# A sum over features before a projection: one fp32 product on TensorE against a split on GpSimd and two ordinary products

## The reference, cut to what matters

```python
def _rmsnorm(x, g):
    xf = x.astype(jnp.float32)
    y = xf * lax.rsqrt(jnp.mean(xf * xf, axis=-1, keepdims=True) + EPS) * g.astype(jnp.float32)
    return y.astype(x.dtype)
...
    x = x + merged @ w_out
    ffn, new_conv = _conv_ffn(_rmsnorm(x, norm_ffn), conv_state, w_up, conv_w, conv_b, w_down)
    x = x + ffn
```

## Time and profile before

| what | us |
|---|---|
| median of 3 runs | 1532.3 |
| lowest, highest | 1532.28, 1532.6 |
| the profiled execution, its own time | 1532.53 |
| its span in the profile | 1530.7 |
| TensorE busy | 1522.8 (99%) |
| VectorE busy | 1025.8 (67%) |
| ScalarE busy | 667.2 (44%) |
| GpSimd busy | 469.4 (31%) |
| granted clock of TensorE, mean | 0.999 |

### The profile page before, as it was taken

One profiled execution on the slowest core, in us unless ns is written; L12 is line 12 of the kernel. 1 busy time (PEld: TensorE's weight loads), 2 busy tenths in 40 slices (PEclk: granted clock), 3 DMA queues, 4 the chain that ended last, 5 costly groups with the idle time before them and its releaser, 6 DMA issues.

```text
span 1530.7 us, 33612 instructions
## 1 busy us (share of the span) xinstructions
PE 1522.8 (99%) x12350; PEld 1508.1 (99%) x12350; DVE 1025.8 (67%) x1479; ACT 667.2 (44%) x903; POOL 469.4 (31%) x608
## 2 busy tenths in 40 slices
PE   9999999999999999999999999999999999999998
PEld 9999999999999999999999999999999999999998
DVE  7655889887667676567777777777777764444443
ACT  7344445454667544444333333333333333333333
POOL 8994468867424101221111111111111100001100
PEclk9999999999999999999999999999999999999999
DMA  8886577676876686565454545454545475555552
GB/s 290 243 200 177 151 223 206 194 215 189 247 218 196 168 212 212 167 213 173 147 183 147 183 147 182 147 182 148 182 147 181 148 224 172 177 173 172 169 178 97
DMA packets 298880, 282.34 MB, mean 184 GB/s; under 512 B 35216, under 2 KB 289312, under 8 KB 298656
## 3 DMA queue, kind: packets, MB, share of 16 engines
q1 hardware_dynamic: 282480, 256.55, 55.8%
q10 hardware_dynamic: 13984, 16.92, 3.5%
q0 software_dynamic: 2320, 7.54, 1.5%
HBM read 266.88 MB, written 14.05 MB: 184 GB/s over the span
## 4 chain that ended last, share of the span: by engine, by line
PE 98%; ACT 0%; ACTq 0%; DMA 0%; issue 0%; DVE 0%; SPq 0%
PE banks L590 31%; PE banks L592 31%; PE banks L591 31%; PE banks L616 2%; PE banks L600 1%; PE banks L831 0%; PE banks L871 0%; PE banks L781 0%; DMA raw<-in_w_u 0%; ACTq L321 0%; PE banks L768 0%; PE banks L884 0%; PE banks L695 0%; PE banks L790 0%; PE banks L843 0%
## 5 line engine op out<-in xcount | busy, mean ns | idle before, releaser
L1396 DVE TENSOR_TENSOR wlo<-raw,whi 128x1024 fp32r<-128x1024 f32 (+1 forms) x442 | 560.5, 1281 | 282.3 <-ACT whi L1008 277.9
L1008 ACT ACTIVATE whi<-raw 128x1024 fp32r<-128x1024 f32 (+1 forms) x442 | 461.1, 1051 | 538.7 <-PE banks L592 490.6
L591 PE MATMUL banks<-h_lo,whi 128*128 128x288 f32 x1408 | 416.0, 295 | 0.0
L592 PE MATMUL banks<-h_hi,wlo 128*128 128x288 f32 x1408 | 415.9, 295 | 0.0
L590 PE MATMUL banks<-h_hi,whi 128*128 128x288 f32 x1408 | 414.9, 295 | 0.0
L591 PEld LDWEIGHTS banks<-h_lo,whi 128*128 128x128 f32 x1408 | 264.7, 188 | 0.1
L592 PEld LDWEIGHTS banks<-h_hi,wlo 128*128 128x128 f32 x1408 | 264.4, 188 | 0.0
L590 PEld LDWEIGHTS banks<-h_hi,whi 128*128 128x128 f32 x1408 | 264.3, 188 | 0.1
L590 PE MATMUL banks<-hhi,whi 128*128 128x288 f32 (+1 forms) x848 | 252.3, 298 | 0.0
L592 PE MATMUL banks<-hhi,wlo 128*128 128x288 f32 (+1 forms) x848 | 250.3, 295 | 0.0
L591 PE MATMUL banks<-hlo,whi 128*128 128x288 f32 (+1 forms) x848 | 250.3, 295 | 0.0
(11 more groups left out here) (360 smaller groups left out, 2227.1 us busy)
## 6 DMA issues: line engine op xcount, KB each, us to landing
raw<-in_w_up SPq DMA_DIRECT2D x352, 256.0 KB, 3.4
raw<-in_w_in SPq DMA_DIRECT2D x208, 256.0 KB, 3.3
raw<-in_w_down SPq DMA_DIRECT2D x176, 256.0 KB, 3.0
raw<-in_w_glu SPq DMA_DIRECT2D x64, 256.0 KB, 3.8
raw<-in_w_out SPq DMA_DIRECT2D x64, 256.0 KB, 3.3
raw<-in_w_attn_proj SPq DMA_DIRECT2D x32, 256.0 KB, 4.1
scratch_gates<-gt ACTq DMA_DIRECT2D x16, 288.0 KB, 3.9
raw<-in_w_u SPq DMA_DIRECT2D x15, 256.0 KB, 5.8
```

The costliest lines, as they stand in the source:

```text
L591: pe.matmul(out, h, xl[:, kt, :], start=False, stop=False)
L592: mm = pe.matmul(out, lo, xh[:, kt, :], start=False, stop=kt == nk - 1)
L1008: act.activation(whi[:, s, :, 0:cols], raw[:, s, :, 0:cols], ACT.Copy).then_inc(hi_ready, 1)
L1396: dve.tensor_tensor(wlo[:, s, :, 0:cols], raw[:, s, :, 0:cols], whi[:, s, :, 0:cols], ALU.subtract).then_inc(lo_ready, 1)
```

## The change

TensorE's one fp32 product with `sqacc` becomes two products of the type fp32r. GpSimd prepares their operands behind its loop: it writes `ones` as fp32r (`ones_r`), copies `sqacc` as fp32r (the high half, `sum_hl[:, 0]`) and subtracts that from `sqacc` (the rest, `sum_hl[:, 1]`). The subtraction counts `sq_done` to 9, and TensorE waits for 9; the later counts move up by one. The two new tiles lie in memory that is free at this time.

```diff
+    sum_hl = at("sum_hl", [P, 2, T], F32R, WK + 30336)
+    ones_r = at("ones_r", [P, P], F32R, WK + 32640)
...
             def token_sums():
 
-                pe.wait_ge(sem("sq_done"), 8)
-                pe.matmul(aux[:, 3, 0:T], ones[:, :], sqacc[:, :], start=True, stop=True).then_inc(sem("sum_ready"), 1)
+                pe.wait_ge(sem("sq_done"), 9)
+                pe.matmul(aux[:, 3, 0:T], ones_r[:, :], sum_hl[:, 0, :], start=True, stop=False)
+                pe.matmul(aux[:, 3, 0:T], ones_r[:, :], sum_hl[:, 1, :], start=False, stop=True).then_inc(sem("sum_ready"), 1)
...
-                        dve.wait_ge(sem("sq_done"), 15)
+                        dve.wait_ge(sem("sq_done"), 16)
...
             own.done(N_OUT)
+            own(copy(ones_r[:, :], ones[:, :]))
+            own.link(copy(sum_hl[:, 0, :], sqacc[:, :]))
+            pool.tensor_tensor(sum_hl[:, 1, :], sqacc[:, :], sum_hl[:, 0, :], ALU.subtract).then_inc(sem("sq_done"), 1)
             pool.wait_ge(sem("sum_ready"), 2)
             own.link(pool.memset(sqacc[:, :], 0.0))
...
-                squares(x3, 2 * k, sq3, 9 + k)
+                squares(x3, 2 * k, sq3, 10 + k)
```

## The result

The changed kernel takes 1535.45 us (median of 12 executions, 1534.47 to 1538.0) against 1532.29 us of the kernel before beside it (12 executions). The ratio is 1.002, with a 95% interval of 1.0012 to 1.0028. The forecast was 1534.4 us, with a range up to 1535.4: the direction is right, the size is 3.2 us instead of 2.1, and the median lies just over the end of the range. The interval means 1.8 to 4.3 us more, so this pair of medians alone does not rule out the forecast of 2.1; the traces and the later executions tell more.

The account below looks back on a forecast made before the run. TensorE, busy for 1522.8 of 1530.7 us, was taken to bound the kernel. A cheaper product (-0.22) and a new stall (+2.35) gave +2.13 us on 1532.3, so 1534.4 us; range 1532.8 to 1535.4.

Parts of the forecast that it names:

- The place and the mechanism: At the sum of squares, TensorE waits for GpSimd's three new instructions, slowed by VectorE's turns: a new stall of 2.35 us.
- The alternation with VectorE: GpSimd and VectorE's line 1396 subtractions take turns, each waiting for the other's whole instruction; the rest ends at 685.93.
- GpSimd's exit from the loop: Idle time between GpSimd's loop of squares and the copy of ones: 0.69 us, bounds 0.08 and 2.79.
- the prediction's own comparison of orders: Other orders of GpSimd's and VectorE's turns end nearly alike: 685.7 with the copy of ones first, 686.14 with VectorE first.
- TensorE's part: At the sum, one fp32 product of 0.49 us gives way to two ordinary ones of 0.27 us: -0.22 us.
- Nothing late behind: Work queued behind the sum, such as the norm's chain, shifts alike and makes no new TensorE wait; room 2.9 us.
- Rival 4: Behind the sum, the norm's chain makes TensorE wait some tenths to 1 us more, 1535 to 1535.5 us; chance 0.07.
- The clock: TensorE's granted clock was expected to stay at 1.00 through the stall at the sum.
- The sum: The forecast's total for the change: -0.22 + 2.35 = +2.13 us, giving 1534.4 us.
- the third rival: TensorE's clock falls in the stall; one piece takes 6.4 us instead of 3.18, together 1537.6 us; chance 0.08.
- Rivals 1 and 2: At the split: no collision, stall 0.8 us, 1532.85 us, chance 0.11; or no stall, net -0.22 us, 1532.1 us, chance 0.04.

Follow-up runs that it names:

- the kernel with TensorE's part alone: Changed kernel without the split: two ordinary products on an operand pre-filled with ones, wait for 8 as before; 1532.14 us, -0.27 against the kernel before.

## Why the prediction was right, and where it fell short

**The place and the mechanism: right, nearly to a tenth.** Moved to the time axis of the trace before (0.65 us earlier), the steps are, forecast and measured: copy of ones done at 683.42 and 683.38; high half at 685.05 and 684.98; the rest at 685.93 and 685.85; stall 2.35 and 2.29 us, counted as the forecast did, from weight load to weight load (686.55 - 0.65 - 683.61). The 2.17 us of the section on the result are counted between products. The alternation with VectorE, read from the earlier trace rows, decided it. Holding VectorE back takes 2.1 of the 2.17 us away, and the shift of the copy of ones moved the stall by 0.5 us as the alternation wants.

**GpSimd's exit from the loop: mis-sized, without effect.** The forecast took 0.69 us from the earlier trace rows; it was 0.23 (the idle time ahead of the copy of ones). The row stood ahead of a transfer's start, and did not carry over to an ordinary instruction. That it had no effect is in part luck: the copy of ones was issued at 682.55, in the same hundredth as VectorE's first subtraction, and came behind it. Had it come first, the end would have moved by 0.2 us only, by the prediction's own comparison of orders (685.7 against 685.93); no run shows that order.

**TensorE's part: right.** 0.26 us for two products instead of 0.49, shown by the kernel with TensorE's part alone. Behind a stall the pair takes 686.93 - 686.56 = 0.37 us, since its second product starts 0.24 us behind the first and not 0.13; so 0.1 of the gain is lost there. Together the sum's place cost 2.17 + 0.37 - 0.49 = 2.05 us against 2.13 forecast.

**Nothing late behind: right.** No new wait of TensorE shows behind the sum in the changed kernel, and none even where the norm chain was started later (one piece later, or VectorE held back). Rival 4 did not come true.

**The clock: wrong.** This is the step that failed. The sum has no term for it, and the third rival had a chance of 0.08, because the clock in the earlier trace rows held for 3 us of idle time. One stretch that holds does not show that a shorter one always will. In the changed kernel the clock fell behind an idle time of 2.2 us: in one of its four profiled executions. Of its 45 executions on all chips, 11 have a mean clock of 0.998, where the kernel before has 1 of 97, and 17 one of 1.000, which leaves at most 28 with one. Of the 45, 23 lie more than 3 us over the median of before; but 13 of the 109 executions of the kernel before lie more than 1 us over theirs, so some of the 23 would lie there without a fall. An estimate from both is that somewhat under half had one. At 1.5 us each that makes 0.7 us more on average, 2.05 + 0.7 = 2.75 us; the executions of the kernel before lie 0.2 us over their own medians on average, which gives 2.95, where the mean of the 45 differences is 2.9. Which execution had a fall was seen only in the profiled ones, and falls occur elsewhere in the program too, as the kernel with TensorE's part alone showed. The price of a fall in the rival was wrong as well: 3.2 us, as a whole piece at half the pace; measured 1.5, since the lower level lasted 3.4 us and products came at 0.24 us instead of 0.133, 1.8 times as far apart and not 2.

The Trainium skill, TensorE: Matmul & The Clock Gate, section Part 1: The HAM clock gate, says that the gate's bookkeeping runs freely, is not reset when a kernel starts, and that the number of slow products at a kernel's start therefore differs from run to run. The traces show the same for a stall in mid-kernel: after the same stall of 2.2 us the clock stayed in the execution of 1534.09 us and fell in the one of 1535.69 us.

**Rivals 1 and 2**, no collision and no stall, are shut out by the rows of 1.48 and 1.64 us. What their gain would have been is seen in the kernel with the sum one piece later: 0.2 us in the trace, nothing in the medians.

## What to carry to other kernels

An operand for the busiest engine that is prepared in several steps on another engine needs room for all of them and for the turns of an engine that it alternates with; here 1.9 us of room met 2.0 us of work and 2.1 us of VectorE's turns. Look for a place one step later before the split is judged: the same code one piece later had no stall. And a short stall on TensorE may cost more than its length: the clock can fall behind it, in some executions only, so a median over few executions says little and the range of a forecast must hold both cases.

## What the hardware showed that was not expected

- The granted clock fell behind an idle time of 2.2 us, when TensorE was at work again: after 0.5 us in one profile, after 1.5 us in another, and in four others it did not fall. Behind a stall of 2.9 us it fell 0.2 us after work was taken up, in a stall of 5.9 us inside it, after 2.3 us, and behind a wait of 2.0 us in the attention part 0.9 us after. At the end of the kernel before it had held for over 3 us of idle time. After a stall of 1.7 us no execution of eleven showed a second group or a mean clock under 0.999.
- At the lower level ordinary products are 0.24 us apart, 1.8 times the 0.133 us at full clock.
- A GpSimd copy to fp32r costs no more than a copy to fp32: 0.67 us for both at 128 x 288, and 0.40 us at 128 x 128, where the two fp32 copies of the earlier trace rows took 0.46 on average.
- GpSimd was idle for 0.23 us when it left its hardware loop for an ordinary instruction; ahead of a transfer's start it was 0.69 us.
